# A late stage that multiplies by squares from the first token group's last ten tiles on, a selection tail that is paced by length, and first operands loaded one stage earlier

## The reference, cut to what matters

```python
xn = rms_norm(h, norm_gain)                  # 2048 x 1024
proj = xn @ w_in                             # 36 column tiles of 128 are left to the late stage
qa, ka, va, ga, qb, kb, vb, gb, iq, ik, iw, za, zb = split(proj)

logits = relu(einsum('bqhd,bsd->bqhs', iqb, ik))      # 8 index heads
score = einsum('bqhs,bqh->bqs', logits, iwb)
score = where(admissible, score, -inf)
_, idx = top_k(score, 256)                   # which keys each query may see
gate_a = sigmoid(za + b_merge[0]); gate_b = sigmoid(zb + b_merge[1])
```

## Time and profile before

| | before |
|---|---|
| median of 3 runs | 4466.68 us |
| profiled execution, its own time | 4470.13 us |
| its span | 4468.2 us |
| TensorE busy | 4134.5 us, 93% of the span |
| VectorE / ScalarE / GpSimd busy | 2469.7 / 1786.7 / 1043.0 us |
| late stage, first to last product | 2245.0 to 3275.5 us of the span |

### The profile page before, as it was taken

One profiled execution on the slowest core, in us unless ns is written; L12 is line 12 of the kernel. 1 busy time (PEld: TensorE's weight loads), 2 busy tenths in 40 slices (PEclk: granted clock), 3 DMA queues, 4 the chain that ended last, 5 costly groups with the idle time before them and its releaser, 6 DMA issues. The chain is left out here.

```text
span 4468.2 us, 65650 instructions
## 1 busy us (share of the span) xinstructions
PE 4134.5 (93%) x23325; PEld 2779.9 (62%) x23325; DVE 2469.7 (55%) x6022; ACT 1786.7 (40%) x3531; POOL 1043.0 (23%) x966
## 2 busy tenths in 40 slices
PE   7899999999967999979889999999879889998998
PEld 5656566666643333335456488888667778777665
DVE  4544444444443333336479867778846655456665
ACT  1233334343310111113258568774247667660000
POOL 0011111111114555532142034444621121000000
PEclk9899999999978999989999999999979989999999
DMA  9765646565507777737464464444553242113331
GB/s 290 243 211 171 202 136 205 150 205 150 192 24 285 275 267 271 265 134 218 141 180 118 130 161 128 147 131 131 161 142 91 62 106 69 46 60 130 121 107 62
DMA packets 661942, 705.64 MB, mean 158 GB/s; under 512 B 195929, under 2 KB 514609, under 8 KB 648689
## 3 DMA queue, kind: packets, MB, share of 16 engines
q1 hardware_dynamic: 570192, 495.68, 37.0%
q0 software_dynamic: 63696, 185.05, 12.1%
q10 hardware_dynamic: 27728, 20.71, 1.4%
HBM read 770.36 MB, written 135.36 MB: 203 GB/s over the span
## 5 line engine op out<-in xcount | busy, mean ns | idle before, releaser
L430 PE MATMUL f_ring<-f_win,f_hT 128*128 128x512 f32 x1024 | 456.0, 601 | 20.0 <-issue 10.3
L430 PEld LDWEIGHTS f_ring<-f_win,f_hT 128*128 128x128 f32 x1024 | 192.0, 191 | 254.6 <-issue 239.5
L1371 PE MATMUL e_ph<-e_gateup,e_rowsT 128*64 128x512 f32 x1536 | 343.3, 600 | 6.4 <-DVE e_rowsT L1538 5.0
L2213 ACT ACTIVATE l_rank<-l_score,l_trial 128x2048 bf16<-128x2048 f32 (+1 forms) x186 | 296.4, 1593 | 28.7 <-DVEq L2313 14.5
L2157 PE MATMUL l_dot<-l_xT,l_w 128*128 128x256 f32 x1152 | 264.7, 385 | 20.2 <-ACT l_dot L2231 16.3
L2774 DVE CUSTOM_DVE_ANT_0 sparse_scores<-sparse_s,sparse_pen 128x512 f32<-128x512 f32 (+3 forms) x320 | 182.8, 609 | 181.5 <-PE sparse_s L126 165.8
L2105 PE MATMUL l_unit<-l_xT,l_w 128*128 128x512 f32 x512 | 247.3, 603 | 33.1 <-DMA l_xT<-mid_xn3T 29.0
L363 POOL TENSOR_TENSOR f_small<-f_small,f_half 128x1 f32<-128x1 f32 (+1 forms) x80 | 51.5, 643 | 891.9 <-DVE f_small L992 307.7
L2157 PEld LDWEIGHTS l_dot<-l_xT,l_w 128*128 128x128 f32 x1152 | 221.9, 193 | 53.7 <-ACT l_dot L2231 18.7
L1371 PEld LDWEIGHTS e_ph<-e_gateup,e_rowsT 128*64 128x64 f32 x1536 | 108.9, 138 | 204.9 <-issue 199.7
L538 PE MATMUL f_ring<-f_wout,f_trio 128*128 128x512 f32 x512 | 226.4, 601 | 1.4 <-DVE f_trio L922 1.4
(11 more groups left out here) (491 smaller groups left out, 8992.3 us busy)
## 6 DMA issues: line engine op xcount, KB each, us to landing
f_win<-in_w_in SPq DMA_DIRECT2D x64, 2048.0 KB, 8.6
l_w<-in_w_in SPq DMA_DIRECT2D x144, 512.0 KB, 4.0
f_win<-in_w_in SPq DMA_DIRECT2D x128, 256.0 KB, 5.0
mid_ys<-e_out SPq DMA_DIRECT2D x48, 512.0 KB, 5.8
f_wout<-in_w_ada SPq DMA_DIRECT2D x20, 1024.0 KB, 12.5
f_win<-in_w_in SPq DMA_DIRECT2D x16, 1024.0 KB, 7.1
mid_gzT<-l_out SPq DMA_DIRECT2D x64, 256.0 KB, 3.4
o_gates<-mid_gzT SPq DMA_DIRECT2D x16, 1024.0 KB, 9.2
```

The lines of the kernel that those rows point to most:

```text
L430: mm = nc.tensor.matmul(to[:, :], hT[:, k, :], w[:, k, :], start=(k == 0), stop=(k == KD - 1))
L1371: mm = nc.tensor.matmul(ph[lane_cols(lane), t % 2, :], xT[:, k, lane_cols(lane)], wgu[:, stream(t, lane), :, k, :], start=(k == 0), stop=( ...
L2213: last = nc.scalar.activation(unread_by_act[:, 0:WIDE[b]], score(b), ACT.Sign, bias=of_block(trial, b).bitcast(F32), scale=-1.0, accum_out ...
```

## The change

There are three parts. (1) `xT` and `w` move into a common buffer, `arena`, which other stages use for tiles of theirs at other times; SyncE loads the late stage's first four weight tiles and first two token groups inside the combine stage, at steps 3, 4, 6, 7 and 5, 9. (2) Only 26 units are left: the last ten column tiles of the first group are done as five quads, so that 59 quads follow instead of 54. The token sums of the first group are formed right after the last `dot`, ahead of the counts, and its `T3` difference behind the last unit, with a semaphore of its own (`x_difference_ready`), for which P7 waits. (3) `select` places selection pieces by their length in elements (a credit of 1500 for each product of a quad), a penalty follows one rank piece later, and the last one is put into the list instead of behind it.

```diff
+ARENA = 12 * D
+def arena(g, at, *shape):
+    flat = g.arena[:, at:at + math.prod(shape)]
...
+LATE_RING = 4
+def late_w_load(g, sp, u):
+    at = LATE[u % len(LATE)][1]
+    sp.dma_start(g.late_w[:, u % LATE_RING, :, :], g.w_in_2[0].rearrange("(k p) n -> p k n", p=P)[:, :, at:at + P]).then_inc(g.late_w_loaded[u % LATE_RING], 16)
+def late_x_load(g, sp, t):
+    sp.dma_start(g.late_xT[:, t % 2, :, :], g.xn3T.rearrange("(k p) t -> p k t", p=P)[:, :, t * 512:(t + 1) * 512]).then_inc(g.late_x_loaded[t % 2], 16)
...
+        LATE_X_AT, LATE_W_AT = (5, 9), (3, 4, 6, 7)
...
                         load(s + 5)
+                    if s in LATE_X_AT:
+                        t = LATE_X_AT.index(s)
+                        for u in range(2):
+                            sp.wait_ge(xT_stored[u], 16 * 2 * (t + 1))
+                        late_x_load(g, sp, t)
+                    if s in LATE_W_AT:
+                        late_w_load(g, sp, LATE_W_AT.index(s))
...
-    UNITS = list(range(NC))
-    QUADS = [(t, c) for t in range(1, TG) for c in range(0, NC, 2)]
+    WHOLE = 26
+    UNITS = list(range(WHOLE))
+    QUADS = [(t, c) for t in range(TG) for c in range(WHOLE if t == 0 else 0, NC, 2)]
...
         def select():
-            if selection:
+            nonlocal room
+            room = min(room, 0.0) + 1500
+            while selection and room > 0:
                 order.append(selection.pop(0))
                 kind, b, j = order[-1]
-                if kind == "rank" and j == 1 and b:
+                if kind == "search":
+                    break
+                room -= length(kind, b, j)
+                if kind == "rank" and j == 2 and b:
                     order.append(("penalty", b - 1, 0))
...
-        return order + [("penalty", NBL - 1, 0)]
+        behind = [e for e, (kind, n, p) in enumerate(order) if kind == "quad" and e > ranked][1:2] or [len(order) - 1]
+        return order[:behind[0] + 1] + [("penalty", NBL - 1, 0)] + order[behind[0] + 1:]
...
-                load_w(0)
-                load_x(0)
-                for u in range(1, WB):
-                    load_w(u)
-                load_x(1)
...
-                load_x(2)
                 load_first()
...
-                    if n == A_GROUP - 1:
-                        load_x(3)
+                    if last_in_group(n) and t + 2 < TG:
+                        late_x_load(g, sp, t + 2)
...
                     elif p == "P7":
+                        pe.wait_ge(x_difference_ready, t + 1)
                         pe.wait_ge(seeded, SEEDED[n, "P6"])
...
-                    V.tensor_tensor(h["T2"], h["B22"], h["T1"], ALU.subtract)
-                    V.tensor_tensor(h["T3"], h["B22"], h["T3"], ALU.subtract)
-                    v.drain().then_inc(x_sums_ready, 1)
+                    V.tensor_tensor(h["T2"], h["B22"], h["T1"], ALU.subtract).then_inc(x_sums_ready, 1)
+
+                def difference_of_x(n):
+                    h = halves(n)
+                    if n == 0:
+                        v.wait_ge(done, WHOLE)
+                    V.tensor_tensor(h["T3"], h["B22"], h["T3"], ALU.subtract).then_inc(x_difference_ready, 1)
...
                     elif kind == "counted":
-                        counted()
+                        v.drain().then_inc(scored, 1)
                         sums_of_x(0)
                         last_sum_of_x(0)
+                        counted()
+                    elif kind == "end" and n == WHOLE - 1:
+                        difference_of_x(0)
```

More of the change, by code:

```diff
@@ L1812, in _ @@
                         residual(s + 2)
-LATE = [(name, W2[name] + c * P, c) for name, n in (("qa", 4), ("ka", 4), ("va", 4), ("ga", 4), ("gb", 4), ("za", 8), ("zb", 8)) for c in range(n)]
 def stage_late(nc, g):
@@ L2855, in stage_output @@
         y = g.branch_in
-        gz = sb("o_gates", [P, 2, KD, W])
+        gz = arena(g, KD * D, 2, KD, W)
         r = sb("o_x", [P, 2, D])
@@ L3134, in build @@
             stage_experts(nc, g)
+            g.late_xT = arena(g, 0, 2, KD, 512)
+            g.late_w = arena(g, 2 * KD * 512, LATE_RING, KD, P)
+            g.late_x_loaded = [x.enter_context(nc.semaphore(f"late_x_loaded_{u}")) for u in range(2)]
+            g.late_w_loaded = [x.enter_context(nc.semaphore(f"late_w_loaded_{u}")) for u in range(LATE_RING)]
             stage_combine(nc, g)
```

79 lines of the change are left out of this document (41 added, 38 removed).

## The result

The changed kernel takes 4428.61 us (median of 4 executions, 4426.06 to 4433.17) where the kernel before takes 4467.75: a ratio of 0.9913, 95% interval 0.9901 to 0.9925, or 39 us less. I had predicted 4406, 61 us less, with a range of 4390 to 4428. The direction was right and the size was not. One execution of all that follow, of the kernel "three edits, wider", took 10708.59 us for a reason that no run shows; it is left out of that kernel's range and ratio.

What follows compares the result with a forecast made beforehand. TensorE was seen as bound by token loads at the late stage's entry, its own products in mid-quads, and VectorE in the tail; 20 + 37 + 4 = 61 us off 4466.7 gave 4406 us, range 4390 to 4428.

Steps and rivals of the forecast that it cites:

- entry: Late stage's start: six loads (6 MB) removed there let TensorE's first products go earlier, 20 us less, bounds 12.8 and 21.8.
- first to last quad product, before the tail: Quads ahead of the tail: stalls of 5 us at quad 0 and 3.6 us at three changes of group.
- tail: Last quads beside VectorE's rank pieces: with pieces spread over 62 products TensorE loses 13 us against 32.1, bounds 0 and 32.
- end: Behind the last product: the last penalty store goes a quad earlier, 4 us less, bounds 2 and 4.5.
- slack: Tail: some 3 us taken off VectorE's 19.5 us lag in reckoning TensorE's loss.
- the slow mixture: Tail: VectorE's rank pieces keep their mixed slow rate, since GpSimd's sums still come once per quad; 120.12 us busy.
- rival B: Entry: TensorE starts early but stands before the first index product until 2248.7; gain 12.8 instead of 20, 4413 us; chance 0.12.
- The changes of group: Quads: three changes of token group instead of two, some 1.2 us each with the slow start, 3.6 us in all.
- rival D: Combine stage becomes bound by its transfers, 86 us show, 4492 us; chance 0.04 with anything ending on its side.
- P7 of quad 0: First quad: this product waits about 3 us for `T3`, with slow products after it 5 us; bounds 0 and 10.
- the 3.83 us for weights: Near 2602: TensorE's wait for a weight load goes, about 6.7 us less with the slow products.
- Rival A: Tail: VectorE's pieces stretch further, spreading gives nothing, 13 becomes 32, 4425 us; chance 0.22 with its half-way forms.

Runs made afterwards that it cites:

- three edits, wider: Changed kernel with mask load ahead of q's, no selection piece at group changes, scans' unused operand from PSUM, and room 1420 instead of 1500: 4409.95 us.
- loads back: Changed kernel with its six first token and weight loads issued at the late stage's start again: 4446.22 us.
- no GpSimd sums: Changed kernel with GpSimd's four weight sums reduced to one sum of 8 columns from quad 45 on: 4404.29 us.
- the fourteen runs: Fourteen further runs that all left the part behind the late stage alone; that part took 1178.4 to 1184.3 us.
- the second profile: The changed kernel itself run once more, nothing changed, to see its tail's spread: 4433.10 us.
- mask first: Changed kernel with GpSimd's 64 KB mask load issued ahead of its eight loads of q: 4430.60 us.

## Why the prediction was wrong

**Step by step.** The profiled execution took 39.3 us less than before; the terms, predicted and measured:

| term | predicted | measured | from |
|---|---|---|---|
| entry | 20 | 15.9 (against "loads back": 13 to 16) | start of the units behind the last index product (2479.72 and 2465.30), less combine's end |
| loads in combine | 0 | 0 | stage 237.5 and 237.8 us, 4.8 of waits in both |
| first to last quad product, before the tail | surplus 8.6 | surplus 11.8 | no GpSimd sums |
| tail | loses 13 | loses 23 to 30 | surplus less 11.8 |
| end | 4 | 4.4 | 12.08 - 7.68 |
| around the late stage | 0 | 4.5 slower | 1.5 ahead of it, 3.0 behind |

Of the 22 us that are missing, the tail has 10 in this profile, the entry 4, the stretch before the tail 3, and the surroundings 4.5. The last row lies within what the fourteen runs showed there, and I count it as spread. By the medians of the two sets of runs the change gives 39.1 and 33.4 us.

**The step that failed first** is the tail: "It falls 19.5 us behind instead of 35. From that go the last piece itself (3.2 us, for which nobody waits any more) and a slack of some 3 us. That leaves **13 us**". The first half was good in this profile: the stretch took 129.0 us against my 126.5, over products of 107; in the other profiles with this pace and both SBUF operands it took 131.9 to 134.8. The second half was not. TensorE lost 23 us, about the whole difference, and 30 in the second profile.

The 6.2 us that I took off assumed that TensorE waits for VectorE alone. In the traces VectorE, GpSimd and TensorE wait for each other in a ring: beside rank pieces one weight sum goes from 1.33 to 2.59 us and a quad's four from 5.33 to as much as 11.3, with 1.7 to 3.6 us to spare; TensorE stands for the sums (10.2 us in the tail), and VectorE then stands for TensorE's products (10.2 us in the second profile).

I had the rule on two SBUF operands in hand, and the row of 1.24 us beside it, and said that the tail then loses 13 us "or more". That row was no witness for the rule on two operands, since its piece reads one SBUF tensor. And I kept "the slow mixture" as a length of VectorE's work and left out what it does to GpSimd, which becomes the one that is waited for. Leaving out the sums removed all of the tail's loss; taking one SBUF operand from the scans removed 11 us of it, about half; spreading the pieces further removed a fifth.

**The entry** was 4 us too high. The first product went when I said (22.1 us earlier, net of combine's end, against 21.8). The mask did not land 2.5 us after its issue but 6.9, where it had taken 12.7 with the 6 MB ahead of it. Its place among GpSimd's own loads is not why: behind four of them instead of twelve ("mask first") it took 6.9 us again, and only its issue came earlier. What made it 6.9 instead of 2.5 stays open. This is rival B halfway. Moving it ahead gave back only 2.3 us, because VectorE's index parts take 6.65 us instead of 4.58 when GpSimd's low part falls beside them; that this is the collision of the tail is likely and not shown by a run of its own.

**The changes of group** were 1.2 us each in my sum. The first one cost 3.52 us of wait and the slow products after it (16 instructions in 5.31 us against 3.62, at a granted clock of 0.53): 5.2 us. I had taken the waits of the two changes of before as the price. It depends on which selection pieces stand on ScalarE and VectorE just there; with none, the wait is 1.32 us.

**What held**: no added wait in combine (rival D is out), P7 of quad 0 (3 us of wait predicted, 1.97 measured), the 3.83 us for weights gone, the end. Rival A, the tail stays VectorE's, is nearest to what happened, at 4425 us, and I had given it 0.22 with its half-way forms.

## What to carry to other kernels

Where two engines stretch each other, read both sides of the collision before pricing a new schedule: moving the same pieces to other places left their total as it was (111.3 and 111.9 us), and the engine that is waited for may change. Taking one of the two SBUF operands away, here one that the operation ignores, was worth more (11 us) than spreading the same work over 62 products instead of 55 (nothing that can be told), and spreading paid only after it (10.7 us, by one profile each). A term for "slack" belongs in the upper bound of a gain, not in its middle.

## What I had not expected of the hardware

- GpSimd's 128x512 sum (the third of a quad's four) needs 1.33 us beside VectorE's one-operand counts and 2.59 us beside the rank pieces; VectorE's scans go from 38.5 to 44.4 us in return, and back to 38.5 once their second operand comes from a column in PSUM.
- The first rank piece has one SBUF tensor as operand and slows all the same, from 11.9 to 16.2 us, while the counting pieces beside GpSimd's 1.33 us sums don't.
- One program's tail differs by 6 us between executions (752.6 and 758.9 us) with identical code, as much as several of the edits are worth.
- A 64 KB load on GpSimd's queue landed 6.9 us after its issue behind twelve other loads and behind four alike, and 12.7 us after it with 6 MB of SyncE's loads under way.
